# Three-pass products over high and low halves for all projections of a two-layer diffusion backbone

## The reference

```python
h = rmsnorm(x, norm_mix_pre) * (1 + sc1) + sh1          # sc, sh, g from silu(c) @ ada_w
z = h @ w_in
z_rwkv = dwconv3(z[..., :o0], rwkv_conv)
gates = sigmoid(z[..., o2:])                            # 3 x 1024
out_a, st_rwkv = rwkv7_branch(z_rwkv, ...)              # bidirectional, 8 heads of 64
out_b = neighbourhood_attention(...) @ w_o_na           # dense attention for the context
out_c, st_ret = retention_branch(z_ret, ...)
merged = gates[0] * out_a + gates[1] * out_b + gates[2] * out_c
x = x + g1 * rmsnorm(merged @ w_out, norm_mix_post)
h2 = rmsnorm(x, norm_ffn_pre) * (1 + sc2) + sh2
u = dwconv3(h2 @ ffn_up, ffn_conv); val, gate = split(u)
x = x + g2 * rmsnorm((gelu(gate) * val) @ ffn_down, norm_ffn_post)
```

## Time and profile before

| | us |
|---|---|
| median of 3 runs (2333.17 to 2338.2) | 2334.23 |
| profiled execution, its own time | 2336.37 |
| span of its instructions | 2334.6 |
| mean granted TensorE clock | 0.952 |

### The profile page before, as it was taken

One profiled execution on the slowest core, in us unless ns is written; L12 is line 12 of the kernel. 1 busy time (PEld: TensorE's weight loads), 2 busy tenths in 40 slices (PEclk: granted clock), 3 DMA queues, 4 the chain that ended last, 5 costly groups with the idle time before them and its releaser, 6 DMA issues. The chain is left out here.

```text
span 2334.6 us, 41014 instructions
## 1 busy us (share of the span) xinstructions
PE 2067.2 (89%) x16984; PEld 1654.9 (71%) x16984; DVE 956.7 (41%) x1589; ACT 854.5 (37%) x1668; POOL 655.7 (28%) x382
## 2 busy tenths in 40 slices
PE   4889999898799969999649898999987999699994
PEld 0466565656599959999605666657565999599994
DVE  2344445444533245560213444444545231555502
ACT  1342333434333344443133423333344333544431
POOL 0010202011155525555202001020201555255551
PEclk9899999999899989999879999999998999899997
DMA  6213222131233313333053131321212433133330
GB/s 241 97 47 109 75 77 97 34 118 44 91 121 126 118 54 126 121 124 127 18 175 116 38 111 63 100 84 65 92 39 92 131 122 117 58 123 127 118 126 28
DMA packets 64405, 227.11 MB, mean 97 GB/s; under 512 B 7264, under 2 KB 11616, under 8 KB 63840
## 3 DMA queue, kind: packets, MB, share of 16 engines
q1 hardware_dynamic: 58464, 215.60, 27.7%
q10 hardware_dynamic: 5760, 8.92, 1.2%
HBM read 220.81 MB, written 3.68 MB: 96 GB/s over the span
## 5 line engine op out<-in xcount | busy, mean ns | idle before, releaser
L415 PE MATMUL psz<-part 128*128 128x386 f32 x5280 | 954.3, 342 | 51.4 <-DVE part L1191 51.0
L415 PEld LDWEIGHTS psz<-part 128*128 128x128 f32 x5280 | 938.8, 190 | 64.0 <-issue 46.2
L1524 POOL TENSOR_TENSOR part<-ring,part 128x1024 fp32r<-128x1024 f32 x220 | 529.0, 2406 | 566.0 <-ACT part L849 566.0
L415 PE MATMUL psz<-hbuf,ring 128*128 128x386 f32 x1344 | 452.4, 494 | 32.0 <-issue 29.3
L415 PE MATMUL psw<-work 64*64 64x64 f32 (+3 forms) x9024 | 398.3, 242 | 43.2 <-ACT work L849 18.5
L415 PEld LDWEIGHTS psw<-work 64*64 64x64 f32 (+2 forms) x9024 | 340.6, 143 | 123.4 <-issue 80.7
L415 PEld LDWEIGHTS psz<-hbuf,ring 128*128 128x128 f32 x1344 | 254.5, 191 | 218.6 <-issue 40.2
L849 ACT ACTIVATE part<-ring 128x1024 fp32r<-128x1024 f32 x220 | 231.6, 1054 | 170.1 <-PE psz L415 153.8
L849 ACT ACTIVATE work<-psw 128x384 f32<-128x384 f32 (+6 forms) x360 | 129.4, 388 | 265.9 <-PE psw L415 224.7
L1524 POOL TENSOR_TENSOR work<-work 128x386 f32<-128x386 f32 (+1 forms) x48 | 42.5, 893 | 440.5 <-DVE work L1191 429.3
L1197 DVE SCALAR_TENSOR_TENSOR mix<-psz,prm,mix 128x385 f32<-128x385 f32 x176 | 109.1, 620 | 136.5 <-ACT mix L849 133.4
(11 more groups left out here) (89 smaller groups left out, 1347.4 us busy)
## 6 DMA issues: line engine op xcount, KB each, us to landing
ring<-in_w SPq DMA_DIRECT2D x400, 512.0 KB, 3.3
pk<-in_pk ACTq DMA_DIRECT2D x8, 832.0 KB, 4.6
const<-in_const SPq DMA_DIRECT2D x1, 2307.0 KB, 8.7
xres<-in_x SPq DMA_DIRECT2D x1, 1544.0 KB, 11.0
out_x<-xres SPq DMA_DIRECT2D x1, 1544.0 KB, 5.1
out_nak<-work ACTq DMA_DIRECT2D x8, 64.0 KB, 1.6
out_nav<-work ACTq DMA_DIRECT2D x8, 64.0 KB, 1.6
out_srt<-work ACTq DMA_DIRECT2D x8, 64.0 KB, 1.5
```

The lines of the kernel that those rows point to most:

```text
L415: ins = nc.tensor.matmul(out, a, b, start=start, stop=stop, skip_group_check=True)
L1524: L.do(G.tensor_tensor(out, a, b, op), S[sig] if sig else None)
```

## The change

All 42 products a layer that were in fp32 become three-pass products. The first two shared blocks and ten blocks of every pair are split like the others: the list `SPLIT` holds all split blocks in order, `j` counts in it. The high half is a copy on ACT (`split(j)`, placed by hand between ACT's steps of the pair), the low half a subtraction on POOL (`low(j)`, placed by hand between POOL's steps), now in place in the ring's slot, which is released only when the product has been done (`read_up`). The halves of h are made once, right after the modulation, and kept for the whole layer (the low half in place in `hbuf`, the high half and `whi` in buffers of their own). For the room, x is stored to its output in DRAM at the head of the layer by ACT's queue and loaded again at the head of the merge; while the pairs run, its place is working memory. SP's loops are written out. In the merge each group runs its six gate products first and its six output products after (`MT`), and the halves of the branch outputs are made in the order 1, 2, 0. The gated residual: ACT scales the product by the gate as it copies it out of PSUM (`gated`, two pieces for the two streams), and DVE's residual is a multiply and an add over two tiles at a time. Three tables of the retention decay become one (`dist`). `normed` runs over the whole width.

```diff
-                MT = [("gate", 0, 0, 0, 0), ("gate", 0, 1, 1, 0), ("out", 0, 0, 2, 0), ("out", 0, 1, 2, 1),
...
+                MT = [("gate", m, b, 3 * m + b, 0) for m in range(2) for b in range(3)]
+                MT += [("out", m, b, 6 + (3 * m + b) // 2, (3 * m + b) % 2) for m in range(2) for b in range(3)]
...
+                    for b in range(RING, BLOCKS):
+                        old = b - RING
+                        if old in SPLIT_OF:
+                            sp.wait_ge(*read_up(SPLIT_OF[old]))
+                        else:
+                            plain += 1
+                            sp.wait_ge(S["w_used"].h, plain)
...
-                    def dense(zi, b, src=h):
-                        out, wt = opened(zi), loaded(b)
+                    def dense(zi, j, src=hsp, wait=None):
+                        out = opened(zi)
+                        pe.wait_ge(S["w_lo"].h, j + 1)
                         for k in range(KT):
-                            mm(out, wt[:, k, :], src[k], k == 0, k == KT - 1, "z_done" if k == KT - 1 else None)
+                            if wait:
+                                pe.wait_ge(S[wait[0]].h, wait[1] + k + 1)
+                            three(out, j, k, src[k], k == 0, k == KT - 1, "z_done" if k == KT - 1 else None)
...
-                    pe.wait_ge(S["h_ready"].h, 2 * KT)
-                    dense(0, SHARED0)
-                    dense(1, SHARED0 + 1)
+                    dense(0, 0, wait=("h_lo", 0))
+                    dense(1, 1)
...
+                            L.settle()
+                            run(hsp[k][0], h[k], sig="h_hi")
...
+                    act.dma_start(x_out, xres).then_inc(S["x_st"].h, 16)
+                    for j in range(3):
+                        split(j)
...
                         for i, dst in enumerate((rc, kc_, vc)):
                             centre_tap(dst, zb + i, "conv", 4 * i + p)
+                            split(sb_ + i + 3)
                         seen(zb + 3)
                         run(nq, z(zb + 3), free=zb + 3, scale=0.125)
+                        split(sb_ + 6)
...
                         act.dma_start(nak[layer, p], nk[:, 0:P]).then_inc(S["out_k"].h, 16)
+                        split(sb_ + 7)
...
                         decays(0)
                         seen(zb + 6)
                         run(mixed[1][p], z(zb + 6), free=zb + 6)
+                        split(sb_ + 8)
                         decays(1)
                         seen(zb + 7)
                         run(tq, z(zb + 7), free=zb + 7)
+                        split(sb_ + 9)
...
                         late_rows(p, zb + 19)
+                        split(sb_ + 10)
...
                         run(ysq, yc, ACT.Square, "ysq_ready")
+                        split(sb_ + 11)
                         retain(5)
                         act.wait_ge(*at_of("gn_done", p, 1))
                         run(yroot, w(3), ACT.Sqrt, "yroot_ready", scale=1.0 / 64, bias=eps_rw)
+                        split(sb_ + 12)
...
+                    act.wait_ge(*at_of("no_ready", PAIRS - 1, 5))
+                    merge_parts(1)
                     act.wait_ge(S["ro_ready"].h, PAIRS)
                     act.wait_ge(S["out_k"].h, 32 * PAIRS)
+                    act.dma_start(xres, x_out).then_inc(S["x_ld"].h, 16)
+                    merge_parts(2)
                     act.wait_ge(S["out_st"].h, 32 * PAIRS)
+                    act.wait_ge(S["o_ready"].h, PAIRS)
+                    merge_parts(0)
...
-                        run(ybuf[m], z(ZO + m), free=ZO + m)
+                        gated(y_out[m], m, ZO + m, gate1)
...
+                        for k in range(0, KT, 2):
+                            y2 = work[:, first + k * TP:first + (k + 2) * TP].rearrange("p (k t) -> p k t", k=2)
+                            x2 = xres[:, k * TP:(k + 2) * TP].rearrange("p (k t) -> p k t", k=2)
+                            for s, _, a, b in STREAMS:
+                                r2 = rstd[:, a:b].unsqueeze(1).to_broadcast([P, 2, b - a])
+                                tt(y2[:, :, a:b], y2[:, :, a:b], r2)
                             L.settle()
                             for s, _, a, b in STREAMS:
+                                tt(x2[:, :, a:b], x2[:, :, a:b], y2[:, :, a:b], ALU.add, sig="x_upd" if s else None)
...
+                    def low(j):
+                        pool.wait_ge(S["w_hi"].h, j + 1)
+                        a = SPLIT[j] % RING
+                        tt(wlo[a], ring[:, a * 1024:(a + 1) * 1024], whi[j % 3].bitcast(F32), ALU.subtract, sig="w_lo")
...
+                    for j in range(5):
+                        low(j)
                     for p in range(PAIRS):
-                        zb = ZP + ZPP * p
+                        zb, sb_ = ZP + ZPP * p, 2 + 10 * p
+                        for j in range(sb_ + 3, sb_ + 7):
+                            low(j)
...
                             tt(ar[:, d, 1, :], rc, Pc, sig="rr_ready")
+                            low(sb_ + 7 + d)
+                        low(sb_ + 9)
...
                             tt(qx[:, d, :], tq[:, LAT:TP], xi[:, d, :], sig="qx_ready")
+                        for j in range(sb_ + 10, sb_ + 13):
+                            low(j)
```

More of the change, by code:

```diff
@@ L54 @@
 BLOCKS = DOWN0 + FT
+SPLIT = [SHARED0, SHARED0 + 1]
+for _p in range(PAIRS):
+    SPLIT += range(PAIR0 + PAIR_BLOCKS * _p, PAIR0 + PAIR_BLOCKS * _p + 10)
+SM = len(SPLIT)
+SPLIT += range(MERGE0, BLOCKS)
+SO, SU, SD = SM + OUT0 - MERGE0, SM + UP0 - MERGE0, SM + DOWN0 - MERGE0
+SPLIT_OF = {b: j for j, b in enumerate(SPLIT)}
 PRM = {}
@@ L247, in trunk @@
         yb, yc, ysq, yroot = scr[4:8]
+        scores = [work[:, at[0] + 384 * i:at[0] + 384 * i + 384] for i in range(2)]
+        ptr = work[:, at[0] + 768:at[0] + 1152].rearrange("p (k q) -> p k q", k=3)
         sdp = wk(2 * 640)
@@ L253, in trunk @@
         sdp = sdp.rearrange("p (h c) -> p h c", h=2)
[L254 to L259, removed]
+        qx = work[:, 3 * TP:3 * TP + 512].rearrange("p (d t) -> p d t", d=2)
+        xi = qx
+        modr = work[:, 8 * 512:9 * 512]
         modr2 = wk(1024)
-        whi = [part[:, i * 1024:(i + 1) * 1024] for i in range(3)]
-        wlo = [part[:, (3 + i) * 1024:(4 + i) * 1024] for i in range(3)]
+        assert at[0] <= WORK, at[0]
         def parts(first, n):
@@ L400, in _ @@
                         sp.dma_start(ring[:, b * 1024:(b + 1) * 1024], wstream[layer, b]).then_inc(w_loaded[b].h, 16)
[L401 to L408, removed]
+                    plain = 0
+                    for b in range(RING, BLOCKS):
[5 more added lines that the diff above has]
+                            sp.wait_ge(S["w_used"].h, plain)
+                        s_ = b % RING
+                        sp.dma_start(ring[:, s_ * 1024:(s_ + 1) * 1024], wstream[layer, b]).then_inc(w_loaded[s_].h, 16)
                 @block.tensor
@@ L864, in root, with gated, modulate @@
                         run(rstd, w(0), ACT.Sqrt, "rt_root", scale=1.0 / D, bias=eps_rms)
-                    def modulate(j, scale, shift, parts=False):
+                    def gated(dst, m, zi, gate):
+                        for s, _, a, b in STREAMS:
+                            run(dst[:, a:b], z(zi)[:, a:b], ACT.Identity, free=zi if s else None,
+                                scale=gate[:, m, s:s + 1], bias=0.0)
+                    def modulate(j, scale, shift):
                         for k in range(KT):
@@ L1624, in constants @@
     x = np.arange(-P, DEC)[None, :] - i[:, None]
[L1625 to L1627 removed]
+    put("dist", x)
     put("xi", np.broadcast_to(np.stack([t + 1, DEC - t]), (P, 2, DEC)))
```

217 lines of the change are left out of this document (105 added, 112 removed).

## The result

The changed kernel takes 2350.78 us (median of 4 runs, 2348.49 to 2353.48) against 2334.11 us (4 runs, 2333.17 to 2338.2) for the kernel before: ratio 1.0068, 95% interval 1.0051 to 1.0086. It is 16.7 us slower; 22.4 were forecast. The profiled span is 2349.7 us against 2334.6, the mean granted clock of TensorE 0.933 against 0.952.

What follows compares the result with a forecast made beforehand. TensorE was taken to set the pace almost everywhere. Terms without the clock gave -2.7 us a layer, -6.4 in all; the clock's +28.8 made +22.4, 2356 us, own range 2340 to 2368 (0.52), eight in ten 2318 to 2380.

Steps and rivals of the forecast that it cites:

- Rival 2: In the pairs, POOL's subtractions don't meet DVE's chain: some -41 us a layer, 2250 us; chance 0.13 (or half of it).
- Part 1: Projections in three passes, on TensorE alone: 42 products a layer save 1.0 us each, 84 in both layers, a ceiling.
- Rival 4: Three passes in a pair cost 5.2 us because of the weights' loads: 2400 us; chance 0.15 together with Rival 3.
- Part 2: Head of a layer to the first pair's lora products: they end at about 96.6 instead of 102.38, -5.8 us a layer.
- Part 3: Start of pairs 2 to 4: DVE and POOL taking turns delay the next group, +4.8 us each, +14.3 a layer.
- Part 4: Second group of a pair: DVE's waits for POOL use up six products' gain; +0.3 us, four times, +1.2.
- the clock term: Half clock behind TensorE's stands: 2.4 us at four a layer, 1.2 at four second groups; +14.4 a layer, +28.8.
- Part 5: Gates at the head of the merge: two done and the third free at 15.7 instead of 26.3 us, -10.6.
- Part 6: Residuals: DVE's updates in halves of two tiles and the scaled copy in two pieces, -1.8 us a layer.
- Rival 1: Turns of DVE and POOL, but no clock loss: -6.4 us, 2328, range 2318 to 2336; chance 0.2.
- Its other reading: TensorE's stands are shorter than 5 us, so no clock loss: -6.4 us, 2328; within Rival 1's chance of 0.2.
- Rival 3: More subtractions met, clock lost at each fifth projection, merge stalls: +40 us, 2375; chance 0.15 together with Rival 4.

Runs made afterwards that it cites:

- kernel with the fills: Changed kernel with POOL's low-half subtraction of 45 pair blocks a layer replaced by three zero fills of the same slot; 2281.52 us, ratio 0.9765.
- the fill: Changed kernel with ten unused fp32 matmuls put on TensorE ahead of the third projection of pairs 2 to 4; 2335.98 us, ratio 1.0004.
- the last version: Changed kernel, POOL waiting for DVE's tail and, before blocks 5 and 6, for kk's square; three low halves moved to DVE; 2292.24 us, ratio 0.9821.

## Why the prediction was right, and where its terms were off

**The mechanism.** Three operations at the start of a pair, each behind one subtraction, and three products in the decays: both were put down in the prediction from the 1.55 and the 3.19 us of the earlier trace rows, and are in the trace (1.70, 2.65, 1.49; 3.22 and 5.41). The kernel with the fills shows that the reads do it. The Trainium skill's rule (SBUF — State Buffer, "Who interferes with whom": contention is with a GpSimd instruction that reads SBUF, "not with one that only writes it") says just that, and the run agrees, with 0.56 beside a fill and 1.70 beside a subtraction. Rival 2 is refuted.

**Part 1, the product.** In a pair too, matmuls start 0.177 us apart (47 of them from 209.74 to 217.88), which is 4.25 us for 24. Rival 4 is refuted.

**Part 2, the head.** -5.8 and the rest of the first stage, -5.3 together; -6.6 measured in the first layer, of which 2 to 3 us can be the scatter named below the table. In the second layer the same terms without the constants, -4.3, stand against a lag that falls from 7.73 to 3.57 (1303.68 to 1307.25), -4.2. In the first, 1.5 is that TensorE's first matmul of all starts at 17.19 instead of 18.66; the smaller table of constants was put at -1. The first product follows the tiles of h from 62.07, and reads low halves of h for which DVE is a bit slower than ACT (stands of 1.24 and 1.31 us); I had the order right and didn't name that.

**Part 3, starts of pairs.** The third projection was to start at T = 16.15; it starts 16.3 us after the pair's first matmul (209.26 to 225.56). The stand was to be 7.6 and is 7.34. With the clock taken out by the fill, the next group starts 29.8 us after the pair's first matmul, where 29.9 was forecast. The clock's 2.4 was too much here: it is 1.5 to 2.5, 2.0 in the mean, because the 4.9 us of low clock in the earlier trace rows were one case, and pair 2 has 3.4. The square of kk was to stand behind one subtraction; what stands behind it is the operation before the square, with one input (below).

**Part 4, the second group.** The maximum was to end at S = 24.2 and ends at 24.2; the mark was to come at S = 41.1, and with the clock term at 42.3, and comes at 41.4 (240.56 to 281.93, with a clock loss inside). Here the step that was off is the clock: "the stand before the fifth projection is in two pieces, 3.7 and 2.6 us". The first piece is there (3.72; it stands before the fourth product and is ended by ACT, not by DVE's maximum), and the clock falls behind it: 15 matmuls in 4.8 us. But the projection that runs at the low clock lies in the time in which TensorE would wait for the maximum: it ends at 264.91, the maximum at 264.73, so it fills what was to be the second stand, and in pair 2 next to nothing is late by it. In pairs 3 and 4 the low clock lasts a little longer, and the mark comes at 41.65 and 41.92. Over both layers the eight second groups exceed the 41.1 by some 4 us, where the clock term put eight times 1.2, or 9.6. This is the largest of the mis-sized terms. It is read from the traces; no run takes the clock loss out of this group alone.

**Part 5, the merge.** The third gate was to start at 15.7 us of the tail (the terms given for it add up to 15.5); it starts 15.8 us after the first gate's first matmul (636.79 to 652.61). The stand, which was to be about 7, is 6.87, ended by ACT's sigmoid. The clock loss behind it is there but smaller than the 2.4 forecast: the low clock lasts 3 us, which costs about 1.5. The stage is 1.5 us a layer better than -8.2.

**Part 6, the residuals.** -1.8 a layer forecast, for both; from the last output product to the first up product the lag falls by 1.5 (5.61 to 4.08, the first up product at 858.15 and 862.23), and in the second residual by 1.8 (6.70 to 4.90), -3.3 together.

**Not foreseen.** Between them, over the FFN, the lag grows by 2.6 (4.08 to 6.70). Here the clock falls a second time, after having risen at about 866:

```profile
862.23 0.66 PE L436 MATMUL psz<-hhi,whi 128*128 128x386 f32 x1 [7.73 <-DVE hlo L1224]
867.71 0.44 PE L436 MATMUL psz<-hhi,whi 128*128 128x386 f32 x1 [0.21 <-DVE hlo L1224]
...
870.59 0.65 PE L436 MATMUL psz<-hhi,whi 128*128 128x386 f32 x1 [0.65 <-DVE hlo L1224]
```

```profile
871.00:874.00 3.00, 3.00 (x11) 3.00 (x11) 1.24 (x2) 1.53 (x2) 0.48 (x1) 0.50 0.30 91
```

The kernel before has the same short stands there and stays at 1.00. The second fall costs about 1.5 of the 2.6. No run isolates what decides it. Nor is the end of a layer settled, 2.8 us. The unforeseen parts (+2.6, +2.8) and the over-priced ones (the clock in the second groups by 5.5 in all, at the pair starts by 2.2, the merge and residuals by 3 a layer) partly cancel. That 22.4 came so near to 16.7 is in part luck; what is not luck is the term for the turns at the pair starts, 14.3 a layer, for which the kernel with the stand filled gives 14.1.

**The rivals.** Rival 1 (turns, no clock loss, 2328) is refuted for the stands of 7 us by the windows at 0.50 and by the fill's 14.8 us, and nearly right for the second group in its result, though not in its reason. Its other reading, stands too short for a drop, fails as well: the clock also fell behind stands of 4.39, 3.72 and 3.38 us. Rival 3 (2375) needed a lost clock that costs at the fifth projection, which is the part of the clock term that came out smallest.

## What to carry to other kernels

Before work is given to an idle POOL, look at what DVE does at that time: a subtraction of 2.4 us that reads SBUF costs a two-input operation of DVE up to its whole length, so it belongs where DVE is in no chain, behind a wait on DVE's own signal, or on DVE itself if that is twice as fast. A saving on the engine that sets the pace is worth only what the next chain leaves of it: with the meetings of DVE and POOL in the pairs gone, 52.5 us came of the 84 saved in products plus some 19 saved elsewhere. Filling a stand with work of no use gave 1.5 to 2.5 us where the clock fell behind it; a slowed stretch that ends in a wait anyway costs little or nothing.

## What the runs showed of the hardware that was not expected

An operation with one tile as its input is not always free of POOL. Here a TENSOR_SCALAR of 386 columns, in the changed kernel, next to a subtraction that runs from 233.24 to 235.65:

```profile
233.55 2.31 DVE L1227 TENSOR_SCALAR work<-work,prm 128x386 f32<-128x386 f32 x1
```

It takes 0.42 in the last version, where POOL waits (227.17), and 0.83 beside a fill from 224.06 to 225.01 (224.40, in the kernel with the fills). The one at the end of the tail takes 0.63 beside a fill (213.32, same kernel) and 0.48 without (222.65, changed kernel). By these two cases it is held up by writes too, while TENSOR_TENSOR is not. A RECIPROCAL of one tile keeps its 2.57 beside a subtraction (211.63).

The clock also fell behind a stand of 3.38 us, in the kernel with the fills: it was 0.93 from 216.30 to 218.00 and 0.50 from there to 221.00, so the fall came some 1.4 us after TensorE had started again at 216.38. Behind the stand of 7.34 us the clock was low from the first matmul. A short stand doesn't protect: in the same kernel, behind the stand of 1.97 us in the second group of pair 3, the clock is 0.50 from 378.20 to 381.40, while behind the same stand in pairs 2 and 4 it stays at 1.00. What tells these cases apart stays open.
